# A spacer of 96 floats ahead of the tokens: every later on-chip buffer begins 384 bytes higher in its partition

## The reference, cut to what matters

```python
def one_block(xb):                                   # 128 tokens
    q = (xb @ w_q).reshape(PEER_BLOCK, PEER_HEADS, 2, PEER_HALF)
    ...
    top_s, pos = lax.top_k(cand_s, PEER_TOPK)        # 16 experts for each token and head
    idx = jnp.take_along_axis(cand_i, pos, axis=-1)
    wts = jax.nn.softmax(top_s, axis=-1).astype(xb.dtype)
    act = jax.nn.gelu(jnp.einsum('thkd,td->thk', u_tab[idx], xb)) * wts
    return jnp.einsum('thk,thkd->td', act, v_tab[idx])
```

## Time and profile before

| | us |
|---|---|
| time, median of 3 runs (3643.76 to 3646.24) | 3645.03 |
| span of the profiled execution, first to last instruction | 3642.9 |
| TensorE matmul busy | 3239.3 (89%) |
| VectorE busy | 2566.0 (70%) |
| ScalarE busy | 1786.9 (49%) |
| GpSimd busy | 876.2 (24%) |

### The profile page before, as it was taken

One profiled execution on the slowest core, in us unless ns is written; L12 is line 12 of the kernel. 1 busy time (PEld: TensorE's weight loads), 2 busy tenths in 40 slices (PEclk: granted clock), 3 DMA queues, 4 the chain that ended last, 5 costly groups with the idle time before them and its releaser, 6 DMA issues. The chain is left out here.

```text
span 3642.9 us, 38191 instructions
## 1 busy us (share of the span) xinstructions
PE 3239.3 (89%) x12808; PEld 2027.9 (56%) x12808; DVE 2566.0 (70%) x5154; ACT 1786.9 (49%) x3858; POOL 876.2 (24%) x778
## 2 busy tenths in 40 slices
PE   6878898898898888888788877889999999999998
PEld 2444344443354434446433222279878989987897
DVE  2577778878887787756877777578666758766665
ACT  2334544544564565444444444355564545555553
POOL 0024344444443445420444444400000000000000
PEclk8999999999999999999899999999999999999999
DMA  9979999999999999982999999966655556565564
GB/s 397 369 282 418 418 419 402 418 420 403 419 398 417 419 419 417 419 323 99 384 416 421 421 421 421 420 220 180 192 167 185 184 177 189 168 189 185 174 186 137
DMA packets 279755, 1157.76 MB, mean 318 GB/s; under 512 B 31059, under 2 KB 33619, under 8 KB 175110
## 3 DMA queue, kind: packets, MB, share of 16 engines
q0 software_dynamic: 110592, 805.36, 53.5%
q1 hardware_dynamic: 168582, 349.73, 29.3%
q10 hardware_dynamic: 384, 0.23, 0.0%
HBM read 1154.07 MB, written 1.15 MB: 317 GB/s over the span
## 5 line engine op out<-in xcount | busy, mean ns | idle before, releaser
L86 PE MATMUL psum<-rows,diag 128*128 128x512 f32 x3072 | 1477.8, 617 | 300.9 <-ACT diag L2245 298.3
L2201 DVE CUSTOM_DVE_ANT_0 rows<-rows,h 128x1024 f32<-128x1024 f32 x768 | 938.9, 1223 | 486.0 <-DMA rows<-in_p_uv,place 483.1
L2097 POOL DMA_INDIRECT rows<-in_p_uv,place x768 | 872.3, 1136 | 1387.6 <-PE psum L86 1077.3
L86 PEld LDWEIGHTS psum<-rows,diag 128*128 128x128 f32 x3072 | 557.1, 193 | 1122.6 <-ACT diag L2245 628.0
L3003 DVE TENSOR_TENSOR weights_low<-landing,weights_high 128x1024 fp32r<-128x1024 f32 x404 | 490.6, 1221 | 296.0 <-ACT weights_high L2950 293.7
L2950 ACT CAST weights_high<-landing 128x1024 fp32r<-128x1024 f32 x402 | 418.6, 1049 | 485.4 <-PE psum L86 340.1
L2232 ACT ACTIVATE acted<-dots 128x1 f32<-128x1 f32 x768 | 155.1, 202 | 870.4 <-DVE dots L2201 867.4
L86 PE MATMUL psum<-weights_high,hT_high 128*128 128x512 f32 x832 | 352.1, 423 | 16.5 <-DVE h L694 6.7
L2245 ACT ACTIVATE diag<-ident,weight 128x128 f32<-128x128 f32 x768 | 308.5, 402 | 70.4 <-ACT weight L2238 0.4
L86 PE MATMUL psum<-weights_high,hT_low 128*128 128x512 f32 x832 | 325.7, 391 | 0.0
L86 PE MATMUL psum<-weights_low,hT_high 128*128 128x512 f32 x832 | 325.6, 391 | 0.0
(11 more groups left out here) (465 smaller groups left out, 3970.7 us busy)
## 6 DMA issues: line engine op xcount, KB each, us to landing
landing<-in_w_in SPq DMA_DIRECT2D x192, 512.0 KB, 3.9
landing<-in_w_ff SPq DMA_DIRECT2D x128, 512.0 KB, 4.3
landing<-in_w_mod SPq DMA_DIRECT2D x48, 1024.0 KB, 9.2
landing<-in_a_w_in SPq DMA_DIRECT2D x64, 256.0 KB
landing<-in_w_br SPq DMA_DIRECT2D x32, 512.0 KB, 4.2
rows<-in_p_uv,place POOLq DMA_INDIRECT x768
lat_landing<-in_b_w_in SPq DMA_DIRECT2D x48, 256.0 KB
landing<-in_a_w_out SPq DMA_DIRECT2D x32, 256.0 KB
```

The source lines that it names most:

```text
L86: return k.nc.tensor.matmul(out, lhsT, rhs, start=first, stop=last)
L2097: k.nc.gpsimd.indirect_dma_start(rows[:, n % ROW_RING, :], None, k.given["p_uv"], bass.IndirectOffsetOnAxis(place[:, g % 4, c:c + 1], 0))\
L2201: V.tensor_tensor_reduce(u, u, token, 1.0, 0.0, ALU.mult, ALU.add, dots[:, g % 4, c:c + 1]).then_inc(dots_done, 1)
```

## The change

One buffer more is allocated between `ones` and `x`. It is named `gap`, has 96 floats (384 bytes) per partition, and nothing reads or writes it. 128 + 384 = 512, so `x` begins at a multiple of 512, and every buffer behind it is 384 bytes higher than before.

```diff
--- before.py
+++ after.py
@@ -3728,7 +3728,7 @@
 
         k.psum = ctx.enter_context(nc.psum_tensor("psum", [P, 8, NC], F32))
         k.modulation = nc.dram_tensor("modulation", (2, DEPTH * 6 * D), F32).ap()
-        with buffers(k, ident=[P, P], ones=[P, P], x=[P, 4, D]) as (k.ident, k.ones, x):
+        with buffers(k, ident=[P, P], ones=[P, P], gap=[P, 96], x=[P, 4, D]) as (k.ident, k.ones, _, x):
             ahead = Kit()
             ahead.small_landed, ahead.chunk_high = sem("small_landed"), sem("chunk_high")
             ahead.chunk_landed = [sem(f"chunk_landed{n}") for n in range(LANDING)]
```

## The result

The changed kernel takes 3610.82 us, the median of 4 runs (3609.97 to 3613.05), against 3645.33 before (4 runs). The ratio is 0.9909 with a 95% interval of 0.9898 to 0.9921: faster by 0.9%, 34.5 us. The forecast of no change was wrong, and the time lies outside its range.

The account below looks back on a forecast made before the run. Transfers were taken to bound 2069 us and PE the last 1283 us. All terms were 0, so 3642.9 + 0 on the span, 3645 us as median of runs, with 3628 to 3656 for 8 in 10.

Parts of the forecast that it names:

- What bounds the kernel: Whole kernel: transfers set the pace in 2069 us, PE in the last 1283 us, neither in 291 us.
- The sensitivity: Gathers: 1 ns on the 2487 ns step is 0.77 us; one per cent on all transfers of the 2069 us, 20.7 us.
- Part (a): Destinations of gathers and weights in the 2069 us, moved from 128 to 0 modulo 512: cost taken as 0.
- I take 0: Gather and weight destinations: no saving taken from aligned writes, since unaligned w_in sources landed no slower than aligned ones.
- the bounds of 0 and 3.0%: Gather and weight writes: saving at most one block in 33, 63 us of the 2069; the lower end was taken.
- The block rule as a rival: Writes in the transfer-bound stages: half-used first block is paid for, 32 us saved, 3613 us (3582 if paid in full); 10 in 100.
- Part (b): Engine reads and writes by PE, DVE and ACT at the new offsets: cost 0, with 6 us either way.
- Part (c): Second network's loads, moved from 384 to 256 modulo 512: gain of 0.1 us each hidden by PE's work, cost 0.
- The slower rival: Ring `rows`: writes and engine reads meet more often, 1% of the rate, 21 us lost, 3666 us; 8 in 100.
- Faster by a little: Picks: writes meet less in memory and hold 423 in place of 420 GB/s, 15 us, 3630 us; 6 in 100.
- It does not do what it says: Second network: buffers end at 256, 288 and 480 modulo 512, not 0; no time of its own, counted in the forecast.
- The range: Whole kernel: 3628 to 3656 us for 8 in 10, reaching from the forecast's own range to the near rivals.

Follow-up runs that it names:

- the ring alone: Kernel before the change, with only the gathers' ring `rows` moved down 128 bytes onto a block: 3614.33 us, ratio 0.9915; mirrored on the kernel after, 3635.84 us.
- the transfers alone: Separate kernel of loads only, no engine at work, varying offsets and row sizes: rows of 8192 bytes ran at 428 GB/s on blocks, 423 and 421 off.

## Why the prediction was wrong, point by point

**What bounds the kernel** was right. The stages said to be paced by transfers lie ahead of the second network, and so does all of the gain; the last stage, said to be PE's, ended with the same 1244.7 us. The sensitivity was right too: 0.77 us for each ns on the step and 20.7 us for each per cent of the transfers. The short stretch shown has the step 32 ns shorter, 25 us, against 25 to 30 for the ring alone; the stage from 273 us on went from 415 to 421 GB/s, 1.4%, which is 30 us on 2069.

**Part (a) failed, at the step "I take 0".** Between the bounds of 0 and 3.0% I chose by the row nearest to the case, and took for it the loads of w_in and w_ff, which differ on the read side. The price is on the written side: 423 against 428 GB/s for the same load with nothing else at work. The text said that this was "the read side and not the write side" and that it settled no small price, and then let it settle one. The other reading stood on the table: in the kernel before no large destination lay on a block, so there was no evidence against a price, and the bound stages would show all of it. In place of 0 the runs show 34.5 us, some 4 ns for each written row.

**The block rule as a rival** had 10 in 100 and the time of 3613 us, 2 from the result. Its time was right and its working was not. It counted the 128 unused bytes of a block at the start, 1.5%. That this comes to nearly the measured time is luck. Nor is the extra block paid in full: that would be 3.0% at 8192 bytes, and 1.2% is measured. The runs show another count: starts at 32 and 224 cost nearly alike, and a start at 128 costs nothing where the row does not touch a further block. With some 4 ns for each row the sum, an estimate, is this: 768 gathers x 8 rows on each DMA engine x 4.4 ns (421 to 427 GB/s in the kernels; at the 3.6 ns of the transfers alone it is 22) = 27 us; 48 loads of w_mod x 8 x 3.6 = 1.4 us; the first layer's 128 mixing loads of 256 KB, 8 rows of 2048 bytes per engine, x 4.0 = 4 us; together 32.5 of 34.5 us. The second layer's 48 mixing loads of 256 KB and 28 of 512 KB, at 4.0 ns for each row of 2048 bytes, are 3.3 us at most, of which a part can be hidden where the DMA share is 0.58. The Trainium skill, "DMA: Bandwidth & Descriptors", section "How a descriptor splits into AXI transactions", has a descriptor split into transactions of 256 bytes at most, each of which starts at a multiple of 256; by that count a row of 8192 bytes at 128 makes 33 where an aligned one makes 32. Writes to the chip and to memory and reads from the chip fit this count: each of them pays at 128. Reads from memory do not, though it is for reads that the section tells the rule: 419 GB/s with the source at 0 and at 128. Its extra beats for the bytes ahead of the start are not seen either: 3651 and 3653 us, where they would give 3619 and 3665 (an estimate from that section).

**Part (b)** was right: L3003 and L2950, the costliest of the second network, take 1220 and 1049 ns after and 1221 and 1049 before; the other groups 391, 396, 1219, 1226 and 1046 after, 391, 395, 1220, 1226 and 1045 before. **Part (c)** was right in its effect. The issues after, which answer to the earlier trace rows, show w_in at the same 3.9 us and w_ff at 3.8 where it was 4.3, and the stage's length did not change:

```profile
landing<-in_w_in SPq DMA_DIRECT2D x192, 512.0 KB, 3.9
landing<-in_w_ff SPq DMA_DIRECT2D x128, 512.0 KB, 3.8
```

**The slower rival** fell: with the first network's buffers at a multiple of 512 the kernel takes 3610.82 us and with them at 256 modulo 512 3610.75, so that meeting at 0 modulo 512 costs nothing, and the phases alone show the price without any engine. **Faster by a little** had the right sign and under half of the size, 15 us; it took the best short rate for the most that writes could reach, 423 GB/s, where 427 was reached. "It does not do what it says" was no matter either, since 256 is enough.

**The range** ended at 3628. With a price bounded only by 0 and 63 us there was no ground for 0 in particular, and it should have taken in the middle of these bounds, 3613.

## What to carry to other kernels

Where transfers set the pace, start each buffer that they write or read on the chip at a multiple of 256 bytes of its partition, with a pitch (the distance from row to row) that keeps every row on it; what matters is that no row touches one block more than its length needs. The price was 4 to 7 ns for each row on its DMA engine, so it is 1% at 8 KB, 5% at 2 KB, 16% at 512 bytes, and over a third for short rows that cross a boundary. A few small buffers or constants at the start of the allocation put everything behind them off the grid, and one spacer, 32 floats here, mends it.

## What the runs showed of the hardware that was not expected

- The price is paid on writes to the chip (428 to 423 GB/s), on reads from the chip (stores, 420 to 406) and on writes to memory (420 to 403), and little or nothing on reads from memory (419 and 419; 3612.8 us with the table shifted, against 3610.8).
- It is for each further block of 256 bytes that a row touches, not for the start: rows of 8064 bytes ran at 426 GB/s from a start at 128 and at 416 from 192.
- A row of 128 bytes that crosses a boundary of 256 bytes brings the rate from 172 to 109 GB/s.
- Why offsets of 32 and 224 cost 5.1 ns a row where 128 costs 3.6 to 4.4, and of 192 with rows of 8064 bytes 7 ns, was not taken apart and stays open. It is seen in the kernels too, as the 6 to 8 us by which the spacers of 104 and 24 floats are slower than the kernel before.
